# Rows of g2 behind the initial-state products, w_out rounded in two quarters and a half, all first w_out halves ahead of the second ones

## The reference, cut to what matters

```
mod   = silu(c) @ w_mod + b_mod            # w_mod 1024 x 6144: six vectors, the last is g2
proj  = (rms_norm(x) * (1 + sc1) + sh1) @ w_in      # w_in 1024 x 2832
att   = grouped attention;  hm = bidirectional mLSTM (decays, initial state C, n, m)
y     = concat(att, sigmoid(o) * rms_norm(hm)) @ w_out      # w_out 1024 x 1024
x     = x + g1 * y
hn    = rms_norm(x) * (1 + sc2) + sh2
gate  = top 8 of 64 experts per token (sigmoid router, 4 of 8 groups)
x     = x + g2 * (sum over experts of gate * down(silu(hn @ w_gate) * (hn @ w_up)) + shared expert)
```

## Time and profile before

| what | value |
|---|---|
| median of 3 runs | 670.17 us (667.8 to 670.3) |
| the profiled execution, its own time | 666.43 us |
| its span, from the first to the last instruction | 664.6 us |
| TensorE busy | 587.3 us, 88% |
| VectorE, ScalarE busy | 211.0 us, 166.6 us |
| data moved by DMA | 252.56 MB, 380 GB/s over the span |
| mean granted TensorE clock | 0.957 of full speed |

### The profile page before, as it was taken

How to read it: one execution, slowest core, us unless ns; L and a number is a source line. 1 busy time by engine, 2 the same in 40 slices (tenths; PEclk the granted TensorE clock), 3 DMA queues, 4 the chain that set the end, 5 groups by cost and what they waited for, 6 DMA issues and landing times.

```text
span 664.6 us, 11043 instructions
## 1 busy us (share of the span) xinstructions
PE 587.3 (88%) x4524; PEld 408.7 (61%) x4524; DVE 211.0 (32%) x471; ACT 166.6 (25%) x296; POOL 29.6 (4%) x76
## 2 busy tenths in 40 slices
PE   0699999979899979999999959699999999857994
PEld 0488787767777546676666735465767666523662
DVE  1287867597822201212121212002221212120113
ACT  3163626751632102121212111011212121210210
POOL 1340210001100000000000000000000000000000
PEclk9979999989999989999999998899999999976998
DMA  8997699927999999999999999999999999999981
GB/s 328 385 347 282 226 365 387 358 84 279 395 420 420 420 421 421 421 421 420 421 421 421 421 422 419 422 420 421 420 422 418 423 418 423 419 421 420 422 341 68
DMA packets 47688, 252.56 MB, mean 380 GB/s; under 512 B 5753, under 2 KB 8961, under 8 KB 22801
## 3 DMA queue, kind: packets, MB, share of 16 engines
q1 hardware_dynamic: 45408, 246.50, 91.2%
q0 software_dynamic: 1840, 4.21, 2.0%
q10 hardware_dynamic: 384, 1.08, 0.4%
HBM read 250.06 MB, written 1.72 MB: 379 GB/s over the span
## 4 chain that ended last, share of the span: by engine, by line
PE 60%; DMA 28%; DVE 5%; ACT 3%; issue 2%; SPq 1%; DVEq 0%; ACTq 0%; POOLq 0%
PE bank L1119 22%; DMA ring<-in_w_up 22%; PE bank L1151 10%; PE bank L1093 6%; PE bank L1130 6%; DMA ring<-in_w_mod 4%; PE bank L779 3%; PE bank L775 3%; PE bank L783 3%; PE bank L720 2%; DMA dec<-max_rows 1%; DMA ring<-in_w_in 1%; DVE w_upper_over L417 1%; PE bank L1058 1%; SPq L481 1%
## 5 line engine op out<-in xcount | busy, mean ns | idle before, releaser
L1119 PE MATMUL bank<-ring,xe 128*64 128x256 f32 (+1 forms) x2048 | 199.8, 411 | 29.9 <-DMA ring<-in_w_up 25.3
L1119 PEld LDWEIGHTS bank<-ring,xe 128*64 128x64 f32 (+1 forms) x2048 | 132.3, 135 | 103.2 <-issue 61.8
L1151 PE MATMUL bank<-ring,actT 128*64 128x512 f32 (+1 forms) x512 | 97.2, 616 | 9.0 <-DMA ring<-in_w_down 5.5
L2046 DVE TENSOR_TENSOR act_e<-bank,sil 128x256 f32<-128x256 f32 x26 | 11.0, 425 | 200.2 <-ACT sil L1504 200.2
L2055 DVE SCALAR_TENSOR_TENSOR ylo<-bank,gslot,yhi 128x512 fp32r<-128x512 f32 x52 | 39.0, 751 | 87.6 <-ACT yhi L1509 87.6
L1509 ACT ACTIVATE yhi<-bank,gslot 128x512 fp32r<-128x512 f32 x52 | 35.8, 688 | 121.8 <-PE bank L1151 121.8
L1504 ACT ACTIVATE sil<-bank 128x256 f32<-128x256 f32 x26 | 10.0, 385 | 215.9 <-PE bank L1119 215.9
L1151 PEld LDWEIGHTS bank<-ring,actT 128*64 128x64 f32 (+1 forms) x512 | 30.0, 129 | 54.6 <-issue 53.7
L1093 PE MATMUL bank<-pone,hhi 128*128 128x256 f32 x204 | 50.8, 287 | 0.0
L1093 PE MATMUL bank<-pone,hlo 128*128 128x256 f32 x204 | 49.9, 282 | 0.0
L1130 PE MATMUL bank<-yhi,ptone 128*128 128x512 f32 x104 | 43.9, 422 | 0.5 <-DVE ylo L2055 0.5
(11 more groups left out here) (330 smaller groups left out, 587.0 us busy)
## 6 DMA issues: line engine op xcount, KB each, us to landing
ring<-in_w_gate SPq DMA_DIRECT2D x64, 1024.0 KB, 18.7
ring<-in_w_up SPq DMA_DIRECT2D x64, 1024.0 KB, 19.6
ring<-in_w_down SPq DMA_DIRECT2D x64, 1024.0 KB, 18.4
ring<-in_w_mod SPq DMA_DIRECT2D x12, 2048.0 KB, 13.4
ring<-in_w_in SPq DMA_DIRECT2D x5, 2048.0 KB, 16.3
ring<-in_w_out SPq DMA_DIRECT2D x2, 2048.0 KB, 14.4
ring<-in_w_in SPq DMA_DIRECT2D x1, 1024.0 KB, 7.6
gb<-g_rows POOLq DMA_DIRECT2D x1, 1024.0 KB, 5.5
```

What stands on the lines that cost most here:

```text
L1119: ins = mm(bank[6][j * w:(j + 1) * w, part * FE:(part + 1) * FE], xe[:, k, slots], weights[:, k, :], start=(k == 0), stop=(k == KD - 1))
L1151: ins = mm(bank[4 + h][j * w:(j + 1) * w, :], actT[:, f, j * w:(j + 1) * w], weights[:, f, 512 * h:512 * h + 512], start=(f == 0), stop=(f ...
```

## The change

The rows of g2 are multiplied right behind `m_initial`, into bank 3 in place of bank 1; `m_values(1)` follows them. Then all four first halves of the w_out products stand together, and the four second halves behind them. The head transposes hm0 stay in the first half of y1_0; hm1 moves into the second half of y0_1, and the turning of the first normalised tokens into the second half of y1_1. ScalarE rounds the first half of w_out in two quarters, and rounds the second half later, behind the rows of g2. VectorE makes the rest of the first quarter ahead of the copies pt1, that of the second quarter between the two `mixed_rest` of attention, and that of the second half behind `add_initial`, which is a part of `heads_out(1)` taken out as a function. SyncE issues the last chunk of g2 ahead of the second half of w_out and no longer waits for that half to land. ScalarE gets a small Sqrt activation behind the sigmoids, which loads the table of that function there.

```diff
@@ the plan of banks
-                    "nd0_0:2 nd0_1:6 nd0_2:5 st1:3 c0:0 c1:4 c2:1 in_0:0 in_1:4 in_2:1 y0_0:7 y0_1:3 "
-                    "nd1_0:2 nd1_1:6 nd1_2:5 y1_0:0 hm0:1 rg2:1 y1_1:4 hm1:2 nT:6 x2T0:5 x2T2:6 rt:1")
+                    "nd0_0:2 nd0_1:6 nd0_2:5 st1:3 c0:0 c1:4 c2:1 in_0:0 in_1:4 in_2:1 rg2:3 nd1_0:2 nd1_1:6 nd1_2:5 "
+                    "y0_0:7 y0_1:3 y1_0:0 hm0:1 y1_1:4 hm1:2 nT:6 x2T0:5 x2T2:6 rt:1")
@@ VectorE, the rest of w_out
-        def rest_of_wout(eng, half):
+        WOUT_PARTS = [slice(0, 2), slice(2, 4), slice(4, 8)]
+
+        def rest_of_wout(eng, part):
 
-            eng.wait_ge(wout_upper, half + 1)
-            v = slice(4 * half, 4 * half + 4)
+            eng.wait_ge(wout_upper, part + 1)
+            v = WOUT_PARTS[part]
@@ SyncE
-                if i == mod_first["g2"] + 1:
-                    load_wout(1, "pj5_1")
-                    sp.wait_ge(wout_loaded[1], 16)
                 load_chunk(i)
+            load_wout(1, "pj5_1")
@@ TensorE
             m_initial()
-
-            def output_half(s, n, half, heads=None):
+            mod_rows("g2")
+            m_values(1)
+
+            def output_half(s, n, half, inside=None):
...
-            pe.wait_ge(wout_upper, 1)
-            pe.wait_ge(wout_rest, 1)
+            pe.wait_ge(wout_upper, 2)
+            pe.wait_ge(wout_rest, 2)
             evacuated(pe, "pv0")
             evacuated(pe, "pv1")
             output_half(0, 0, 0)
             output_half(0, 1, 0)
-            m_values(1)
-            output_half(1, 0, 0, heads=0)
+            output_half(1, 0, 0, lambda: m_out_transposes(0))
+            output_half(1, 1, 0).then_inc(wout_half_used, 1)
+            pe.wait_ge(wout_upper, 3)
+            pe.wait_ge(wout_rest, 3)
             evacuated(pe, "hm0")
-            mod_rows("g2")
-            pe.wait_ge(wout_upper, 2)
-            pe.wait_ge(wout_rest, 2)
             complete("y0_0", output_half(0, 0, 1))
-            complete("y0_1", output_half(0, 1, 1))
-            output_half(1, 1, 0, heads=1).then_inc(wout_half_used, 1)
+            complete("y0_1", output_half(0, 1, 1, lambda: m_out_transposes(1)))
...
             complete("y1_0", output_half(1, 0, 1))
-            turn_tokens(0)
-            complete("y1_1", output_half(1, 1, 1))
+            complete("y1_1", output_half(1, 1, 1, lambda: turn_tokens(0)))
@@ ScalarE
             upper_wout(0)
+            upper_wout(1)
             rows_out("m1")
...
-            upper_wout(1)
             for s in range(NST):
                 evacuated(act, f"pj5_{s}")
                 A(og[:, s, :], og[:, s, :], ACT.Sigmoid).then_inc(o_sig, 1)
+            A(table_load[:, :], ones[:, 0:1], ACT.Sqrt)
...
             head_root(0)
+            rows_out("g2")
+            upper_wout(2)
             heads_transposed(0)
-            rows_out("g2")
             head_root(1)
@@ VectorE
+            def add_initial():
+
+                for i in range(3):
+                    ps = product(dve, f"nd1_{i}")
+                    evacuated(dve, f"in_{i}")
+                    drain(f"nd1_{i}", V.tensor_tensor(of_block(kw, i), of_block(kw, i), block_of(ps, i), ALU.add))
...
             ins.then_inc(kw_ready, 1)
+            rest_of_wout(dve, 0)
             for b in (2, 3):
...
             mixed_rest("pv0", 0)
+            rest_of_wout(dve, 1)
             mixed_rest("pv1", 1)
-            rest_of_wout(dve, 0)
             decay_scores(1)
             heads_out(0)
-            rest_of_wout(dve, 1)
+            add_initial()
+            rest_of_wout(dve, 2)
             mixed_rest("hm0", 0)
             heads_out(1)
```

More of the change, by code:

```diff
@@ L966, in output_half @@
                 for k in range(4 * half, 4 * half + 4):
-                    if heads is not None and k % 4 == 2:
-                        m_out_transposes(heads)
+                    if inside is not None and k % 4 == 2:
+                        inside()
                     mm(ps[:, :], mixed_hi[:, k, tok], wout_hi[:, k, w], start=(k == 0), stop=False)
@@ L1429, in heads_transposed, with upper_wout @@
                 drain(f"hm{s}", A(mixed_hi[:, 4:8, s * P:s * P + P], ps[:, :].rearrange("p (a b) -> p a b", a=4), ACT.Copy))
-            def upper_wout(half):
-                act.wait_ge(wout_loaded[half], 16)
+            def upper_wout(part):
+                act.wait_ge(wout_loaded[part // 2], 16)
                 act.wait_ge(chunk_used, last_use[mod_first["m1"]])
-                if half == 1:
+                if part == 2:
                     product(act, "rm1")
-                v = slice(4 * half, 4 * half + 4)
+                v = WOUT_PARTS[part]
                 A(wout_hi[:, v, :], wout[:, v, :], ACT.Copy).then_inc(wout_upper, 1)
@@ L1813, in heads_out @@
                     for i in range(3):
-                        evacuated(dve, f"in_{i}")
-                        ins = V.tensor_tensor(of_block(kw, i), of_block(kw, i), block_of(ps[i], i), ALU.add)
-                        drain(f"nd1_{i}", ins)
                         evacuated(dve, f"nd1_{i}")
```

## The result

The changed kernel takes 664.15 us in the median of five runs (662.84 to 665.88), the kernel before 668.91 us beside it (667.8 to 670.3): a ratio of 0.9921, with a 95% interval of 0.9898 to 0.9944. By the ratio that is 5.3 us less, where 5.5 were forecast. The profiled execution of the changed kernel took 665.88 us, its span is 664.0 us and its mean granted clock 0.955.

What follows compares the result with a forecast made beforehand. The expert stream bounds the kernel; its start waits for the early load and the router's way. Gain 194.5 - 188.0 - 1.0 = 5.5 us, so 666.43 - 5.5 = 660.9 profiled; median, 3.7 higher, 664.7; range 660.5 to 668.7.

Steps and rivals of the forecast that it cites:

- C: Stretch from the first refill's issue to the end of the span; the prediction expected the same work in the same order.
- A: Stretch from SyncE's first request behind the last projection to the last residual's end; forecast 5.5 us shorter.
- B: Stretch from the last residual's end to the first refill's issue; the prediction rests on a profile with 21.59 us.
- The dip: Expert stream behind the first refills: stands 1.0 us, from 213.0 to 214.0, until the last early pair of refills flows.
- The early load: First expert tiles issued at 136.4 instead of 152.9, 16.5 us earlier; DMA then idle about 10 us before the first refill.
- Rival 2: Whole early start of the expert load carries through: 16.5 us less, 653.7; partial form 8.2 us, 662.0; chance 0.08.
- The chunk of g2: Second chunk of g2, issued ahead of w_out's second half, lands by 129.3; if late, it costs TensorE 2.5 us.
- masks: Start of VectorE's first operation on the decays, awaiting the decay maxima load, counted from SyncE's first request behind the last projection.
- The clock: TensorE's granted clock 1.00 from 130 to 165 us; first refill near 186.3, prediction wrong if later than 188.
- rival 1: Part of the shift is lost on the router's way, nearest cause a 1.7 us TensorE clock fall: 666.4 us; chance 0.22.
- Rival 3: w_out's second half lands at 142 or later and holds the router's way: gain about 1.5 us, 668.7; chance 0.10.
- rival 4: Expert stream runs dry between refill pairs, each restarting the flow: 2.0 us slower, 672.2; chance 0.05.

Runs made afterwards that it cites:

- late load: Changed kernel, but SyncE issues the first expert tiles only when y0_0 is complete: 665.59 us, 0.9937 of the kernel before.
- two with fillings: Changed kernel with 16 unread transposes ahead of the second turning of tokens, 663.14 us; with 14 more ahead of the chosen experts' products, 661.82 us.
- no Sqrt: Changed kernel without the small Sqrt activation that fetches the table early: 664.25 us, 0.9931 of the kernel before.
- g2 alone: Kernel before with g2's rows behind `m_initial`, SyncE's new order and g2's copy out behind the sigmoids; rounding, w_out halves and VectorE as before: 669.79 us, 1.0001.
- the filled kernel before: Kernel before with 14 transposes that nobody reads in TensorE's gap ahead of the chosen experts' products: 668.03 us, 0.9985 of the kernel before.

## Why the prediction was right

**One point decides, when the refills flow: right.** Over all 14 profiles C is 471.8 to 474.8 us while A + B goes from 70.3 to 77.9, and the medians follow A + B, all but that of the late load. C hides that DMA idles ahead of the first refill in one kernel and has work left in the other. The kinds of loss were right; two of the three sizes were not, and they cancel. By the first refill 60.8 MB have been moved in the profile of before and 62.2 in the changed kernel, so 1.5 MB, 3.5 us, stood in the queue, not 2.7. The restart cost 1.5 us (issue at 190.44; 20 GB/s up to 192, then 406), close to 1.7. The dip came near 217, later than 213 because the first refill was, and it was twice as long as forecast: 293 GB/s in 216 to 220 is 1.2 us and 322 in 220 to 224 another 0.9, 2.1 in place of 1.0. So 3.6 us are lost against a backlog of 3.5, forecast 2.7 against 2.7. That the gain of the stream still equals the router's shift is luck in the sizes.

The Trainium skill (DMA: Bandwidth & Descriptors, "Anatomy of one DMA") gives about 2.0 us as the fixed cost of a DMA on GpSimd's path, most of it for the landing to be confirmed. These loads are SyncE's, and their restart took 1.5. The prediction's estimate of 4.9 us from the page's figure is a slip: with 2.0 for both restarts its own sum gives 5.2 (flow from 188.3, ten tiles through at 213.3, restart at 214.3).

**The early load: right.** Tiles went out 20.3 us behind the request, forecast 19.6. Some 10 us of idle DMA were forecast, some 11 seen. Rival 2 is excluded by it, and by the late load: 16 us of earlier load are worth 0.9 to 1.6 us.

**The chunk of g2: right in what happens, its bound too small.** It was there in time, and with the old order it would have cost 4.2 us at its place, not 2.5, and the whole gain of 5. This was the most valuable line of the change, and the prediction gave it a subordinate clause.

**VectorE: right to half a microsecond.** The first quarter was hidden; it ended 6.2 us behind the request (6.1 forecast). The decayed scores came 3.7 to 3.9 us earlier (4.05 forecast), the rest of the second half waited 0.61 us for ScalarE (1.0 forecast), the last heads were ready 0.7 us behind the forecast.

**What bounds A: right, with more room than was counted.** The prediction had TensorE without a wait from 132.75 to 160.3, with no slack at the root and 0.6 us at hm1. TensorE is busy without a break from 134 to 160, and 0.9 us of delay at the root changes nothing. A was forecast to end 47.9 us behind the request and ends at 48.5 to 48.7, so its shift is 4.9 us and not 5.5. It follows the masks alone: A less masks is 38.77 to 38.81 in six profiles with the new order (two of the changed kernel, two with fillings, late load, no Sqrt), and 43.98 to 44.04 in four of the order before. The change of order is so worth 5.2 us at equal masks, of 5.5 forecast; the other 0.3 no run explains.

**The rest of the miss is the load of the decay maxima.** It took 9.28 us in the changed profile, 8.83 before, and pushed `m_initial` behind it (the wait of 0.24 us on ScalarE's proj). The masks start at 9.43 to 9.96 in the changed kernel and its variants and at 9.38 to 9.52 in those of the kernel before. The request for w_out's half now shares the queue with a chunk at that time, but the kernel with g2 alone does the same and has 9.42. This cause stays open; it is worth 0.3 us.

**The clock: wrong.** It was to be 1.00 from 130 to 165, and it was; but its fall from 168 to 178 put the first refill at 190.44, behind the 188 at which the prediction called itself wrong, and 189.47 in the second profile is behind it too. (The flow behind it, 417 GB/s from 192 to 645, is over the 415 of the other sign.) The step that failed is the baseline: it took the B of one profile, 21.59, as the kernel's, and with it the router's way. It did not look at the gap of 1.58 us at 180.61 in that same profile, and rival 1 was weighed as a loss of the changed kernel alone, at the 1.7 us of a fall that lay off the path. Both kernels have a gap of 1.6 to 1.8 us on the way to the refill and lose 1.2 to 2.8 us behind it in four of their five profiles, so it cancels in the ratio. Nothing in the prediction says why it should: that part is luck. Had the clock fallen in one kernel only, the error would have been as large as that loss. The step from the profile to the median was luck too: the 3.7 us between them came from three runs of before, whose median fell from 670.17 to 668.91 with two more, and 5.5 less than that is 663.4; the forecast was 664.7, the measurement 664.15.

**Rivals 3 and 4.** Rival 3 did not occur, but something close to it does when the rows of g2 are moved alone, and takes the whole gain. Of rival 4 one dip of 2.1 us was seen, where a single pair of refills was 1.0 us late by the forecast; the second and third profiles of before have one at 220 to 224 as well (330 and 328 GB/s).

## What to carry to other kernels

The parts of such a change don't add up: without the quarters 2.8 us are lost, without the new order of SyncE 5.0, and the rows of g2 alone give nothing, for a total of 5. Where two limits lie within 3 us of each other, price each part against both, and look first at what each queue waits for at the moment of the move. And before a gain of half a per cent is read off two profiles, take each kernel's profile more than once and compare distances between events, stretch by stretch, at the same clock.

## What the runs showed of the hardware

A gap on TensorE of only 1.58 to 1.80 us can be followed by 3 to 10 us at 1.2 GHz, and need not be: of the same gaps in the same program some were followed by a fall and others were not, and a gap of 2.93 us in the filled kernel before was followed by none. The Trainium skill (TensorE: Matmul & The Clock Gate, Part 1) ties the clock to how busy the engine has been lately; the traces agree in that every fall seen from 118 to 206 us comes with a gap or right behind one, of 1.58 to 3.97 us, and that with both gaps of the router's way filled there was none from 120 to 240 us. They don't tell which gap is followed by one. And 30 transposes whose results are thrown away cost no time that could be seen, since they stand where TensorE waits.
